# The projections of a hybrid layer rewritten: tiles in pairs by Strassen's product on half of the inner tiles, and the pairs of one head laid between the attention steps of another

## The chip, the cores and the metric

One core of one Trainium2 chip runs the kernel. The metric is the device time of one execution in microseconds (us). The time before is the median of three runs. The profiler recorded one further execution, and all rows below are of that one.

## The reference, cut to what matters

The input x is 2048 rows of 1024 numbers. One large product gives all inputs of four branches, and one gate of 1024 columns for each of them:

```python
proj = x @ w_in                       # 2048 x 1024 by 1024 x 9216
q_sb, k_sb, v_sb, g_sb, u_pool, g_pool, u_lru, g_lru, q_xa, g_xa, merge = split_columns(proj)
y_sb   = stick_breaking_attention(q_sb, k_sb, v_sb) * silu(g_sb)     # 4 heads of 128, causal
y_pool = multiscale_pool(u_pool, w_pool, pool_scale) * silu(g_pool)  # windows 2, 4, 8, 16
y_lru  = rg_lru(u_lru, ...) * silu(g_lru)                            # convolution, two gates, a scan
y_xa   = memory_cross_attention(q_xa, mem, w_mem_kv) * silu(g_xa)    # 256 memory rows
merged = sum(sigmoid(merge[n]) * (y[n] @ w_branch[n]) for n in range(4))   # 512 x 1024 each
out = layer_norm(ALPHA * x + merged @ w_out, ln_g, ln_b)
```

The attention makes for a block of 128 queries and all earlier blocks of keys the scores z, then log(1-sigmoid(z)), its sums over all later keys, and from them the weights of the values.

## The kernel before

The 2048 rows are done in two halves of 1024 (T); a half is two column blocks of 512 (C) in the moving operand. Everything is held turned, features on the partitions. A float32 product is made as three products of a finer and a coarser part: the high part is the number rounded to fp32r (ScalarE, a copy), the low part the rest (a subtraction, on VectorE or GpSimd). So XH and XL hold the half of x in 8 inner tiles, WH and WL hold one weight tile of 1024x128, and `product` runs 8 inner tiles times 3 passes times 2 blocks of 512 = 48 matmuls into two PSUM banks for one tile of 128 output columns. There are 72 such tiles in a half, taken in an order written out by hand: 16 for the heads of the attention (q, k, g, v of each), 8 gates, 8 for the pools, 8 gates, 8 for the recurrence (LRU), 8 gates, 8 for the memory attention, 8 gates. After each group of gates comes `merge`: a product of the gates' tile, then `branch`, 24 matmuls of the branch's output with w_branch, and GT and MERGED collect gate times branch on VectorE and GpSimd. The half ends with `merged @ w_out`: 8 row blocks times 2 column parts, 24 matmuls each (L662).

ScalarE splits each weight tile one tile ahead (L679), GpSimd makes its rest (L1457), SP loads the tile after that into RAW. The consumers read the PSUM banks directly, each with the operation that it needs anyway (sigmoid, scaling, high part).

The attention of a head is 12 steps in the first half and 28 in the second. A step on TensorE is three matmuls of scores (L446), two of sums (L459, L461), two of the carry to the next block (L470, L472) and one float32 product with the values (L489, two records). Step s makes the scores of block s, the sums of s-3, the values of s-4. Between them lie four activations on ScalarE, four or five operations on VectorE, one or two on GpSimd. The first steps are laid between the head's last product tile; the rest runs with no products beside it. The first products of the next head start when the last values are done.

The output weights are split while the last gates' product runs: `split_out` for the first four tiles stands in ScalarE's `merge` ahead of the last gate's sigmoid, into memory (WO0H, WO0L) that no running product reads.

TensorE takes its instructions in order, and so does each other engine. Semaphores carry every dependence.

Of the kernel before, what the change touches and what calls it, by code (L numbers as in the profile page):

```python
# [11 lines left out]
P = 128  # L12
# [5 lines left out]
C = 512  # L18
# [12 lines left out]
XP = 8  # L31
# [5 lines left out]

SET_EXP_TANH, SET_SIGMOID, SET_SQRT, SET_EXP_LN = 0, 2, 3, 6

# [3 lines left out]
PER_HALF = 4 * HEADS + 3 * 2 * HEADS + NB * FT + FT  # L43
# [7 lines left out]

POOL_OUT = [(g + 1) % 2 for g in range(4)]

SUMS, USE, EARLY = 3, 4, 4


def wait_if(engine, semaphore, count):

    if not (isinstance(count, int) and count <= 0):
        engine.wait_ge(semaphore, count)


def each(engine, first_too, n, body):


    if first_too:
        body(0)
    with engine.Fori(1 if first_too else 0, n) as i:  # L70
        body(i)


def steps_of(half):


# [8 lines left out]

def build(nc, xt, xrow, memt, w8, w4, wgate, wpool, prm, cst, ln_g, ln_b, out):
    with ExitStack() as ctx:
        base = (nc.sbuf_base + 31) // 32 * 32

        def at(name, offset, shape, dt=F32):  # L90
            return nc.alloc_sbuf_tensor_at(name, [P] + shape, dt, offset=base + offset)
# [4 lines left out]
        KIB = 1024  # L96

        XH = at("XH", 0, [KD, T], F32R)
        XL = at("XL", 32 * KIB, [KD, T], F32R)
        YH = at("YH", 64 * KIB, [KB, T], F32R)  # L100
        YL = at("YL", 80 * KIB, [KB, T], F32R)
        RAW = [at(f"RAW{i}", (96 + 4 * i) * KIB, [KD, P]) for i in range(2)]
        WH = [at(f"WH{i}", (104 + 4 * i) * KIB, [KD, P], F32R) for i in range(2)]
        WL = [at(f"WL{i}", (112 + 4 * i) * KIB, [KD, P], F32R) for i in range(2)]
        BRAW = [at(f"BRAW{i}", (120 + 2 * i) * KIB, [KB, P]) for i in range(2)]
        BH = [at(f"BH{i}", (124 + 2 * i) * KIB, [KB, P], F32R) for i in range(2)]
        BL = [at(f"BL{i}", (128 + 2 * i) * KIB, [KB, P], F32R) for i in range(2)]
        R1, R2, RC = 132 * KIB, 164 * KIB, 204 * KIB + 64
        IDENT = at("IDENT", RC, [P])
        SUFFIX = at("SUFFIX", RC + 512, [P], F32R)  # L110
        CARRY = at("CARRY", RC + 1024, [P], F32R)
        DIAG = at("DIAG", RC + 1536, [P])
        COUNT = at("COUNT", RC + 2048, [len(WINDOWS), HALO])
        PRM = at("PRM", RC + 2304, [KB, P_ALL])
        GP = at("GP", RC + 2464, [P_ALL])
        HSTATE = at("HSTATE", RC + 2528, [KB])
        LHALO = at("LHALO", RC + 2560, [KB, 4])
        PHALO = at("PHALO", RC + 2624, [KB, HALO])
        SM = at("SM", RC + 2880, [32])
        SM2 = at("SM2", RC + 3008, [64])  # L120
        STATS = at("STATS", RC + 3264, [TB, 12])


        MERGED = at("MERGED", R1, [FT, T])

        E = [at(f"E{i}", R1 + 2 * i * KIB if i < 2 else 126 * KIB, [C]) for i in range(3)]
        PF = [at(f"PF{i}", R1 + (4 + 2 * i) * KIB, [C]) for i in range(2)]
        PHI = [at(f"PHI{i}", R1 + (8 + 2 * i) * KIB if i < 3 else R2 + 36 * KIB, [C], F32R) for i in range(4)]
        PLO = [at(f"PLO{i}", R1 + (14 + 2 * i) * KIB if i < 3 else R2 + 38 * KIB, [C], F32R) for i in range(4)]
        ARG = [at(f"ARG{i}", R1 + (20 + 2 * i) * KIB, [C]) for i in range(4)]  # L130
        W = [at(f"W{i}", R1 + (28 + 2 * i) * KIB, [C]) for i in range(2)]
        VT = at("VT", R1 + 28 * KIB, [T])
        CRAW = at("CRAW", R1 + 28 * KIB, [C_ALL])
        MRAW = at("MRAW", R1 + 4 * KIB, [KD, MEM])
        MTH = at("MTH", R1 + 12 * KIB, [KD, MEM], F32R)
        MTL = at("MTL", R1 + 20 * KIB, [KD, MEM], F32R)
# [1542 lines left out]
```

## Time and profile before

| | |
|---|---|
| median of 3 runs | 2672.77 us (2671.5 to 2676.21) |
| the profiled execution's own time | 2669.68 us |
| its span | 2667.9 us |
| TensorE matmul | 2596.8 us busy, 97% |
| TensorE weight load | 2080.3 us, 78% |
| VectorE, ScalarE, GpSimd | 1072.6, 902.7, 1025.7 us |
| matmuls in the profile | 11360 |
| mean granted clock | 0.995 |

A matmul's recorded duration is longer than its place in the stream, since the next one starts while it drains. What one costs is the distance between two starts. A gap shorter than the draining doesn't show as idle time, so the span is compared with the count of matmuls too.

### The profile page before, as it was taken

The numbers are of one execution on the slowest core, as the hardware profiler recorded it, in microseconds if no ns is written. First come the engines' busy times: TensorE is split into PE (matmuls) and PEld (weight loads), VectorE is DVE, ScalarE is ACT, GpSimd is POOL, SyncE is SP. The second block draws the span as 40 slices with busy tenths as digits, with TensorE's granted clock in tenths as the row PEclk, the third lists the DMA queues.
The fourth block names the chain that finished last, engine by engine and source line by source line (L and its number), as shares of the span: only waits on it lengthen the run. The fifth ranks groups of instructions, "written<-read, shape, count | busy, mean of one in ns | idle before, by whom it ended". The sixth has DMA issues, their size and how long they took to land.

```text
span 2667.9 us, 31598 instructions
## 1 busy us (share of the span) xinstructions
PE 2596.8 (97%) x11360; PEld 2080.3 (78%) x11360; DVE 1072.6 (40%) x1701; ACT 902.7 (34%) x1496; POOL 1025.7 (38%) x654
## 2 busy tenths in 40 slices
PE   8999999999999999999999999999999999999998
PEld 7777788778877878887767767688878877888887
DVE  5545400520372034046576484701420471143056
ACT  4444411111252133122576584711121351132132
POOL 3443443433234313326344353633443234322425
PEclk9999999999999999999999999999999999999999
DMA  5111111111112111133201101011111112111131
GB/s 218 48 56 47 66 53 36 54 50 40 44 44 63 35 44 58 52 134 117 89 32 31 39 16 55 16 47 36 56 56 39 36 44 63 38 55 50 47 134 64
DMA packets 51629, 153.40 MB, mean 58 GB/s; under 512 B 5856, under 2 KB 11488, under 8 KB 51552
## 3 DMA queue, kind: packets, MB, share of 16 engines
q1 hardware_dynamic: 41472, 133.50, 15.2%
q10 hardware_dynamic: 10080, 18.88, 2.0%
q8 instruction: 48, 0.79, 0.1%
q14 instruction: 29, 0.24, 0.0%
HBM read 136.10 MB, written 16.25 MB: 57 GB/s over the span
## 4 chain that ended last, share of the span: by engine, by line
PE 81%; DVE 11%; ACT 2%; issue 2%; POOL 2%; ACTq 0%; POOLq 0%; DVEq 0%
PE PJ L399 50%; PE Z L526 7%; PE OB L526 3%; PE ACC L526 3%; PE PJ L662 2%; PE OB L489 2%; DVE XC L1317 2%; PE PJ L446 2%; PE PJ L489 1%; PE Z L446 1%; DVE PS L1275 1%; PE Z L662 1%; DVE RES L1441 1%; PE PJ L459 1%; DVE LT L1331 1%
## 5 line engine op out<-in xcount | busy, mean ns | idle before, releaser
L399 PE MATMUL PJ<-XH,WH 128*128 128x512 f32 x2304 | 715.1, 392 | 4.2 <-DVE XL L1060 4.2
L399 PE MATMUL PJ<-XL,WH 128*128 128x512 f32 x2304 | 710.8, 390 | 0.0
L399 PE MATMUL PJ<-XH,WL 128*128 128x512 f32 x2304 | 710.4, 390 | 0.0
L1457 POOL TENSOR_TENSOR WL<-RAW,WH 128x1024 fp32r<-128x1024 f32 x136 | 329.3, 2422 | 881.4 <-ACT WH L679 881.4
L399 PEld LDWEIGHTS PJ<-XH,WH 128*128 128x128 f32 x2304 | 431.1, 188 | 97.0 <-issue 8.4
L399 PEld LDWEIGHTS PJ<-XL,WH 128*128 128x128 f32 x2304 | 433.3, 188 | 90.6
L399 PEld LDWEIGHTS PJ<-XH,WL 128*128 128x128 f32 x2304 | 432.9, 188 | 90.4
L766 ACT ACTIVATE GT<-PJ 128x512 f32<-128x512 f32 x128 | 69.5, 595 | 564.0 <-PE PJ L399 564.0
L1112 DVE TENSOR_TENSOR GT<-Z,GT 128x512 f32<-128x512 f32 x64 | 41.3, 687 | 523.3 <-PE Z L526 523.3
L1533 POOL TENSOR_TENSOR PLO<-PF,PHI 128x512 fp32r<-128x512 f32 (+3 forms) x160 | 179.1, 1119 | 112.3 <-DVE PHI L1183 112.3
L679 ACT CAST WH<-RAW 128x1024 fp32r<-128x1024 f32 x134 | 140.5, 1049 | 130.7 <-PE PJ L399 130.5
L1508 POOL TENSOR_TENSOR MERGED<-MERGED,GT 128x1024 f32 (+1 forms) x62 | 150.0, 2420 | 55.6 <-DVE GT L1112 55.6
L1112 DVE TENSOR_TENSOR GT<-ACC,GT 128x512 f32<-128x512 f32 x32 | 22.1, 692 | 366.3 <-PE OB L526 366.3
L1461 POOL TENSOR_TENSOR BL<-BRAW,BH 128x512 fp32r<-128x512 f32 x64 | 82.2, 1290 | 135.3 <-ACT BH L691 135.3
L691 ACT CAST BH<-BRAW 128x512 fp32r<-128x512 f32 x64 | 39.0, 622 | 245.4 <-PE Z L526 167.2
L1477 POOL TENSOR_TENSOR ML<-MERGED,MH 128x1024 fp32r<-128x1024 f32 x28 | 68.1, 2432 | 95.4 <-ACT MH L1002 95.4
L815 ACT ACTIVATE W<-ARG 128x512 f32<-128x512 f32 (+3 forms) x160 | 89.1, 561 | 36.0 <-DVE ARG L1163 26.9
L489 PE MATMUL OB<-W,V 128*128 128x512 f32 (+2 forms) x192 | 89.0, 545 | 4.9 <-ACT W L815 4.7
L804 ACT ACTIVATE E<-E 128x512 f32<-128x512 f32 (+3 forms) x160 | 90.7, 567 | 5.4 <-issue 1.6
L670 ACT ACT_TABLE_LOAD x67 | 86.0, 1283 | 12.6 <-PE OB L608 11.5
L798 ACT ACTIVATE E<-E 128x512 f32<-128x512 f32 (+3 forms) x160 | 89.3, 558 | 0.3
L526 PE MATMUL Z<-YH,BH 128*128 128x512 f32 x256 | 80.4, 396 | 5.7 <-POOL BL L1461 5.7
(338 smaller groups left out, 3948.8 us busy)
## 6 DMA issues: line engine op xcount, KB each, us to landing
RAW<-w SPq DMA_DIRECT2D x156, 512.0 KB, 3.5
BRAW<-w SPq DMA_DIRECT2D x64, 256.0 KB, 3.2
XRAW<-xt SPq DMA_DIRECT2D x16, 512.0 KB, 10.6
RES<-xrow SPq DMA_DIRECT2D x16, 512.0 KB, 7.8
out<-RES SPq DMA_DIRECT2D x16, 512.0 KB, 2.6
MW<-w SPq DMA_DIRECT2D x8, 512.0 KB, 8.5
k_keep<-KH ACTq DMA_DIRECT2D x4, 512.0 KB, 2.7
k_keep<-KL ACTq DMA_DIRECT2D x4, 512.0 KB, 3.5
```

The source lines that it names most:

```text
L399: mm = nc.tensor.matmul(PJ[p][c][:], w[p][:, k, :], x[:, k, c * C:(c + 1) * C], start=(k == 0 and n == 0), stop=(k == KD - 1 and n == 2))
L489: nc.tensor.matmul(OUT[c][:, a:C], V[:, b, :], W[r % 2][:, a:C], start=first, stop=end, skip_group_check=True).then_inc(pv_done, 1)
L526: mm = nc.tensor.matmul(BR[p][c][:], w[p][:, k, :], y[:, k, c * C:(c + 1) * C], start=(k == 0 and m == 0), stop=(k == KB - 1 and m == 2))
L670: act.add_instruction(mybir.InstLoadActFuncSet(name=nc.get_next_instruction_name(), engine=mybir.EngineType.Activation, act_func_set_id=nu ...
L679: nc.scalar.copy(WH[p][:], RAW[p][:]).then_inc(w_hi, 1)
L798: nc.scalar.activation(e, e, ACT.Exp, scale=-1.0).then_inc(exp_done, 1)
L804: nc.scalar.activation(e, e, ACT.Ln, bias=1.0).then_inc(ln_done, 1)
L815: nc.scalar.activation(W[r % 2][:, a:C], ARG[r % 4][:, a:C], ACT.Exp).then_inc(w_done, 1)
L1457: G_.tensor_tensor(WL[p][:], RAW[p][:], WH[p][:].bitcast(F32), ALU.subtract).then_inc(w_lo, 1)
L1461: G_.tensor_tensor(BL[p][:], BRAW[p][:], BH[p][:].bitcast(F32), ALU.subtract).then_inc(b_lo, 1)
L1508: G_.tensor_tensor(d, d, GT[p][:], ALU.add).then_inc(merged, 1)
L1533: G_.tensor_tensor(PLO[s % 4][:, a:C], PF[s % 2][:, a:C], PHI[s % 4][:, a:C].bitcast(F32), ALU.subtract).then_inc(p_lo, 1)
```

## The change

**Pairs.** Two weight tiles are done together as a pair; there are 36 in a half. The inner dimension is cut: the first four inner tiles (x: B11, B12 over B21, B22; weights: the same four blocks of two tiles) go by Winograd's form of Strassen's product, seven block products of 6 matmuls; the other four inner tiles go plainly, 48 matmuls. A pair is 15 pieces of 6 matmuls, 90 in all, where two tiles took 96. Four sums of x are made once a half (T1 to T4, GpSimd), four sums of weights for every pair (`sums_raw`, GpSimd). The sums of the results are made outside TensorE: a bank that has been used in one result is copied to memory by ScalarE (`shared`, four times a pair), is accumulated further, and VectorE adds another bank to the copy (`summed`, four times a pair). The results of a pair so lie in memory, and what was made of the banks directly (sigmoid, high part) is now an operation of its own from memory.

```diff
+            def piece(g, i):                      # TensorE
+                a, c, d = (J[(g + j) % 3] for j in range(3))
...
+                if i == 0:
+                    pe.wait_ge(w_lo, 4 * g + 1)
+                    wait_if(pe, ad_done, 4 * (g - 1) + 2)
...
+                    block_product(a, ONE, 0, B11, True).then_inc(pr_done, 1)
...
+                elif i == 9:
+                    pe.wait_ge(cp_done, 4 * g + 3)
+                    block_product(a, SUMMED, 4, T3, False).then_inc(pr_done, 1)
...
+            def piece(g, i):                      # ScalarE
+                if i == 0:
+                    second_tile(g)
+                    room(g, 0)
+                    shared(g, 0, 0, 0, 1)
...
+                elif i == 9:
+                    shared(g, 1, 0, 0, 6)
+                    if not last:
+                        sums_of(g + 1)
...
+            def piece(g, i):                      # VectorE
+                if i in (4, 8, 12, 14):
+                    summed(g, (4, 8, 12, 14).index(i))
...
+            def piece(g, i):                      # GpSimd
+                if i == 0:
+                    second_tile(g)
+                elif i == 4 and not last:
+                    first_tile(g + 1, False)
+                    sums_raw(g + 1)
+                elif i == 8 and not last:
+                    first_tile(g + 1, True)
+                elif i == 9:
+                    sums_of(g + 1)
```

**Attention.** q, k and v of a head are written to device memory and are loaded again (`load_kq`, `load_v`, on ScalarE's queue) when its attention starts; splitting them is done then (`split_kq`, `rest_kq`). The attention of head h runs while the two pairs of head h+1 are made: four pieces before the first step, the others spread evenly over the steps. The last head has only the first pair of the gates. The scores have three banks in place of four.

```diff
+                for g, i in fill[:filled(half, h, -1)]:
+                    piece(g, i)
+                for s in range(ns + USE):
+                    if 0 <= s - SUMS < ns:
+                        sums(half, h, s - SUMS)
+                    if s < ns:
+                        scores(half, h, s)
+                    for g, i in fill[filled(half, h, s - 1):filled(half, h, s)]:
+                        piece(g, i)
+                    if s >= USE:
+                        values(half, h, s - USE)
+                    if 0 <= s - SUMS < ns:
+                        carry(half, h, s - SUMS)
```

**The other stages.** The work of the head before is called at set pieces of the running pair. In the memory attention:

```diff
+                # TensorE
+                    pair(g0 + XA0 + h, {9: lambda: memory_turned(half, h - 1),
+                                        12: lambda: memory_values(half, h - 1)} if h else {})
+                    memory_scores(half, h)
+                # ScalarE
+                    hooks = {9: lambda: memory_queries(half, h), 12: lambda: load_memory_values(half, h)}
+                # VectorE
+                    return {3: lambda: memory_max(half, h), 7: lambda: memory_norm(half, h),
+                            10: lambda: (silu(half, 3, h, AG[h % 2][:]), memory_turned(half, h)),
+                            13: lambda: memory_output(half, h)}
...
+                    hooks[8] = lambda: memory_queries(half, h)
```

On TensorE the hook stands ahead of its piece, on the others behind it. `memory_turned` on TensorE turns the weights into PSUM, on VectorE it copies them out (four copies of 512); `memory_values` waits for the last of these. `memory_queries` on VectorE waits for ScalarE's `memory_queries`, which stands behind `shared` and `sums_of` of piece 9.

**Output weights.** They now lie where x and its sums lie (0 to 64 KiB), so ScalarE's `split_out` waits until all products of the half are done; tiles 4 to 7 are loaded when tiles 0 to 3 have been split, since there are four raw buffers:

```diff
+                    act.wait_ge(pr_done, 8 * PAIRS * (half + 1))
+                    nc.scalar.copy(WO[k // 4][0][:, :, (k % 4) * P:(k % 4 + 1) * P], OR[k % 4][:]).then_inc(wo_hi, 1)
...
+                for k in range(FT):               # ScalarE
+                    split_out(k)
                 table(SET_SQRT)
+                split_rows(0, slice(0, 6))
...
+                    else:                         # SP, k >= 4
+                        sp.wait_ge(wo_odd if k % 2 else wo_even, half * 4 + (k - 4) // 2 + 1)
...
+                for f in (6, 7):                  # GpSimd, end of merge
+                    rest_b(half, n, f)
+                    if n:
+                        add(half, n, f - 2)
+                if n:
+                    add(half, n, 6)
+                    add(half, n, 7)
...
+                for k in range(1, FT, 2):
+                    rest_out(half, k)
```

VectorE makes the rests of the even tiles and then those of the rows. `merged @ w_out` now goes row block by row block, both column parts of one behind each other. The x of the second half is split by ScalarE in 11 units of 1024 columns (8 before), as before only after the last row product of the first half. The branches' outputs are split in four operations of 1024 columns once a branch, low parts on VectorE. Loops over heads and gates are unrolled.

## Rows read from the trace of the kernel before

**Rows 1.** The page: the span, and TensorE's busy time, share and instructions.
```profile
span 2667.9 us, 31598 instructions
PE 2596.8 (97%) x11360; PEld 2080.3 (78%) x11360; DVE 1072.6 (40%) x1701; ACT 902.7 (34%) x1496; POOL 1025.7 (38%) x654
```

**Rows 2.** Timeline of PE, product tiles: start, duration, instruction, records merged (x2).
```profile
1399.79 0.61 PE L399 MATMUL PJ<-XH,WH 128*128 128x512 f32 x2
...
1411.58 0.62 PE L399 MATMUL PJ<-XH,WL 128*128 128x512 f32 x2
```

**Rows 3.** Timeline of PE where the output product starts, first half.
```profile
1179.60 0.39 PE L526 MATMUL OB<-YH,BL 128*128 128x512 f32 x1
1179.83 0.39 PE L662 MATMUL PJ<-WO0H,MH 128*128 128x512 f32 x1
1180.06 0.39 PE L662 MATMUL PJ<-WO0L,MH 128*128 128x512 f32 x1
```

**Rows 4.** Timeline of PE: first product of a head, two heads of each half.
```profile
107.62 0.71 PE L399 MATMUL PJ<-XH,WH 128*128 128x512 f32 x1
180.51 0.47 PE L399 MATMUL PJ<-XH,WH 128*128 128x512 f32 x1
...
1387.46 0.70 PE L399 MATMUL PJ<-XH,WH 128*128 128x512 f32 x2
1498.71 0.47 PE L399 MATMUL PJ<-XH,WH 128*128 128x512 f32 x1
```

**Rows 5.** Timeline of PE: the value products of two attention steps in the second half.
```profile
1442.05 1.02 PE L489 MATMUL PJ<-W,V 128*128 128x512 f32 x2
...
1444.54 1.02 PE L489 MATMUL PJ<-W,V 128*128 128x512 f32 x2
```

**Rows 6.** Timeline of PE: float32 value products of the memory attention, four records each.
```profile
967.11 1.88 PE L608 MATMUL ACC<-PT,VM 128*128 128x512 f32 x4
968.82 1.88 PE L608 MATMUL OB<-PT,VM 128*128 128x512 f32 x4
```

**Rows 7.** Waits of PE: for whom, us in total, times, longest.
```profile
PE Z L576 <- POOL PLL L1573: 9.2, 5, 3.1
PE Z L595 <- DVE XCL L1327: 7.5, 8, 2.2
```

**Rows 8.** Timeline of PE from the last row product to the second half's products.
```profile
1269.80 0.39 PE L662 MATMUL OB<-WO1H,ML 128*128 128x512 f32 x1
...
1272.92 0.70 PE L399 MATMUL PJ<-XH,WH 128*128 128x512 f32 x2 [2.74 <-DVE XL L1060]
```

**Rows 9.** A window behind that gap: busy us of each engine, granted clock, DMA.
```profile
1274.00:1278.00 4.00, 4.00 (x12) 3.14 (x11) 4.00 (x4) 3.95 (x5) 0.00 (x0) 0.57 0.02 4
```

**Rows 10.** The page's groups: busy us, mean ns of one, idle before.
```profile
L1457 POOL TENSOR_TENSOR WL<-RAW,WH 128x1024 fp32r<-128x1024 f32 x136 | 329.3, 2422 | 881.4 <-ACT WH L679 881.4
...
L766 ACT ACTIVATE GT<-PJ 128x512 f32<-128x512 f32 x128 | 69.5, 595 | 564.0 <-PE PJ L399 564.0
...
L679 ACT CAST WH<-RAW 128x1024 fp32r<-128x1024 f32 x134 | 140.5, 1049 | 130.7 <-PE PJ L399 130.5
...
L670 ACT ACT_TABLE_LOAD x67 | 86.0, 1283 | 12.6 <-PE OB L608 11.5
```

**Rows 11.** Groups of VectorE with their shapes apart.
```profile
L1060 DVE TENSOR_TENSOR XL<-XRAW,XH 128x1024 fp32r<-128x1024 f32 x16 | 23.1, 1502 | 1.6 <-POOL RES L1612 1.4 <-ACT XH L718 0.2
...
L1399 DVE COPY PT<-Z 128x512 f32<-128x512 f32 x16 | 10.2, 681 | 0.0
...
L1347 DVE SCALAR_TENSOR_TENSOR LR<-LR,LT 128x1024 f32<-128x1024 f32 x8 | 9.8, 1226 | 0.3
```

**Rows 12.** Groups of GpSimd with their shapes apart: a subtraction of 256 columns.
```profile
L1547 POOL TENSOR_TENSOR WL<-RAW,WH 128x256 fp32r<-128x256 f32 x32 | 23.8, 742 | 0.0
```

**Rows 13.** DMA issues: KB of one, median us from issue to landing.
```profile
RAW<-w SPq DMA_DIRECT2D x156, 512.0 KB, 3.5
...
V<-v_keep ACTq DMA_DIRECT2D x4, 512.0 KB, 5.6
```

More of the change, by code:

```diff
@@ L404, in _, with pair @@
+            def pair(g, inside={}):
+                for i in range(PIECES):
+                    if i in inside:
+                        inside[i]()
+                    piece(g, i)
             for h in range(HEADS):
@@ L450, in sums @@
[L450 to L459 removed]
+                    pe.wait_ge(kq_lo, kq_count(half, h))
@@ new lines, in memory_values @@
+            def memory_values(half, h):
+                hh = half * HEADS + h
+                pe.wait_ge(pt_done, 4 * (hh + 1))
+                pe.wait_ge(vm_back, 16 * (hh + 1))
+                for c in range(NC):
+                    for m in range(MEM // P):
+                        mm = nc.tensor.matmul(BR[1][c][:], VM[:, m, :], PT[c][:, m, :], start=m == 0,
+                                              stop=m == MEM // P - 1)
+                    mm.then_inc(xo_done, 1)
+            for half in range(HALVES):
+                g0 = half * PAIRS
+                pair(g0)
+                pair(g0 + 1)
+                for h in range(HEADS):
@@ new lines, in attention @@
+            def attention(half, h):
+                ns, fill = NS[half], filling(half, h)
+                rest_kq(half, h)
+                if h:
+                    output(half, h - 1, 1)
+                silu(half, 0, h, ST[(half * HEADS + h) % 3][:])
+                for g, i in fill[:filled(half, h, -1)]:
+                    piece(g, i)
+                for s in range(ns + USE):
+                    if 0 <= s - SUMS < ns:
+                        argument(half, h, s - SUMS)
+                    if s == ENDS[half][0] + USE + 1:
+                        output(half, h, 0)
+                    if 1 <= s <= ns:
+                        softplus(half, h, s - 1)
+                    if s:
+                        for g, i in fill[filled(half, h, s - 2):filled(half, h, s - 1)]:
+                            piece(g, i)
@@ new lines, in pair, with x_sums @@
+            def pair(g, after={}):
+                for i in range(PIECES):
+                    piece(g, i)
+                    if i in after:
+                        after[i]()
+            def x_sums(half, j):
+                b11, b12, b21, b22 = XRAW[:, 0:2, 0:C], XRAW[:, 0:2, C:T], XRAW[:, 2:4, 0:C], XRAW[:, 2:4, C:T]
+                t = [x[:] for x in TR[half]]
+                for k in (0, 1) if j == 0 else (2, 3):
+                    pool.wait_ge(x_in[k], 16 * (half + 1))
+                if j in (1, 3):
+                    pool.wait_ge(t_raw, 4 * half + (1 if j == 1 else 2))
+                a, b = ((b12, b11), (b22, t[0]), (b22, b12), (b21, t[1]))[j]
+                G_.tensor_tensor(t[j], a, b, ALU.subtract).then_inc(t_raw, 1)
@@ L1550, in attention @@
[L1550 to L1565 removed]
+                ns, fill = NS[half], filling(half, h)
```

2434 lines of the change are left out of this document (1309 added, 1125 removed).

## The prediction

> **What bounds the kernel now.** The first look is the page's busy shares [rows 1]: TensorE is busy 97% of the span and nothing else is above 40%. So time can only be won by giving TensorE less to do or by closing its gaps. The second look is its timeline, for what one matmul costs. From 1399.79 to 1411.58 us there are 26 groups of two [rows 2], that is 52 matmuls in 11.79 us, 0.2267 us each; a tile of 48 takes 10.88. Where the output product starts, three passes into one bank follow each other at 0.23 us too, and the first stands 0.23 behind the last branch matmul [rows 3]: passes into one bank are no slower than passes into two, and that transition has no gap.
>
> The third look is at the heads. From first product to first product a head takes 72.9 us in the first half and 111.3 in the second [rows 4]. A full attention step there is 2.49 us long [rows 5]. Its slots on TensorE are seven times 0.2267 and one float32 product; two of those take 1.71 us [rows 6], one 0.855, so the sum is 2.44. VectorE and ScalarE have four operations of about 0.6 to 0.7 us a step each (such widths in [rows 10, 11]), so the step runs at the edge of three engines. By slots a first-half head is four tiles (43.5), six full steps (14.7) and six narrow ones (an estimate by their widths, with none under 1.0 us: 8.2), 66.4 us; a second-half head is 43.5, 22 full steps (53.7) and 8.2, 105.4. The differences, 6.5 and 5.9 us, are the ramp and the drain of the attention, which has nothing beside it. Over eight heads that is 50 us.
>
> The fourth look is at the waits: in the pool and LRU stages TensorE waits for chains of VectorE and GpSimd, 9.2 and 7.5 us in all [rows 7]. Last, between the halves TensorE stands still for 2.74 us while the new x is split [rows 8], and behind it four microseconds have a granted clock of 0.57 [rows 9], which is nearly all at 1.2 GHz. Half of that time is lost, about 1.6 us: I add it to every gap longer than some 2.5 us.
>
> **The sum, term by term, against the span of 2667.9.**
>
> *A, fewer matmuls.* 36 pairs a half lose 6 matmuls each: 72 x 6 x 0.2267 = -97.9 us. Nothing else on TensorE gets shorter; the turning of v, branches, attention and output have as many matmuls as before.
>
> *Can the others feed it?* A pair is now 20.4 us of TensorE, 1.36 a piece. ScalarE has for it two casts of 512 columns, one of 1024 (1.05) and one of 768 (0.8), and four copies of 0.6 [rows 10]: 5.5 us. VectorE has four additions out of PSUM at about 0.69 each, near the 0.68 of such a copy [rows 11]: 2.8. GpSimd has 1.3 + 1.3 + 2.4 + 1.8 us of rests, by columns from 2.42 [rows 10], and four sums of 0.74 [rows 12]: 9.8. The tightest wait inside a pair is that for WLS: piece 9 done, copy 0.6, cast 1.05, rest 2.42, with hand-overs 4.3 us, against six pieces (8.2) until TensorE wants it. A weight tile lands 3.5 us after its issue [rows 13]; it has at least half a pair. So the plain pairs cost nothing beyond their slots, and additions and copies are hidden by matmuls. If that cover were gone, each pair would lose the difference.
>
> *B, the attention.* Steps now hold 1.7 pieces on average in the first half (about 4.7 us a step) and 0.84 in the second (3.6), so VectorE's and ScalarE's 2.5 us are covered and the drain lies under the next head's pieces. What is new is the reload. ScalarE issues it when the last scores are made; two or three tiles of 512 KB land in some 6 to 7 us (from 3.5 for one [rows 13]), the high parts take 1.05 each, and the last low part 1.2 more. That is 11 to 13 us, against 13.5 (second half) to 17 of TensorE's remaining values, sums and four lead pieces. It fits, but ScalarE then still has a sigmoid, two table loads (1.28 each [rows 10]), one split and two copies ahead of the first magnitude: some 2 us late for each of three heads in the second half. With the first head of a half (the copy of the turned v stands before the next pair, 1.3) and the last heads (only 15 pieces, 2 to 3) I count 13.5 us left of the 50, after which the first product of a merge follows. Term: -36.
>
> *C, the memory attention, a new wait.* Take piece 9 of a pair done. ScalarE copies the bank (0.6), casts the summed weights (1.05) and scales q (1.05); only then can VectorE make q's low part (1.23 [rows 11]). VectorE's queue holds that ahead of the silu (1.23) and of the four copies of turned weights (4 x 0.68 = 2.7) for which `memory_values` waits. With 0.3 for hand-overs the last copy is done 8.2 us behind piece 9. TensorE has pieces 10 and 11, 2.7 us, and waits 5.5, behind which come 1.6 for the clock. What is queued behind it is everything: pieces 12 to 14 and the next scores. This holds for three pairs a half (in the fourth no q stands between): 6 x 7.1 = +42.6. The waits of this stage before (some 3 us a half, q's low part and a little) go: -6. Term: +37.
>
> *D, the output weights, a new wait.* After the last pair TensorE has four branches, 21.7 us. Count from that pair's end. GpSimd's queue puts the last addition to MERGED, which waits for the last branch, ahead of its first rest: 23.3 to 25.8. Two rests are done at 28.3 and 30.7; only then is tile 7 loaded into tile 3's buffer: landed 34.5, cast by ScalarE 35.6. Then ScalarE's table load 36.9, the cast of six eighths of a row block 37.8, VectorE's rest of that 38.8, hand-overs 0.5. TensorE stands still from 21.7 to 39.3, 17.6 us, and 1.6 for the clock. Before, the same place had no gap [rows 3]. Term: 2 x 19.2 = +38.
>
> *E, between the halves.* Before 2.74 and 1.6 us [rows 8, 9]. Now pieces 3 and 4 want five and seven units, which come at VectorE's 1.2 us each while a piece takes 1.36: 2.5 at the start, 2 in between, 2 more for the last unit, which stands behind the last row's normalisation. Term: +2.5.
>
> *F, pools, LRU, merges.* The chains of [rows 7] are as long as before, but begin a few pieces earlier. By my count VectorE's windows make the third and fourth pool pairs late by 1 to 2.5 us; each LRU pair is late by about 1.5 (convolution, silu and variance stand ahead of its last addition) and the second gates' pair behind the LRU by 2.4, since its copy goes where the scan's data lie. Some 30 us where the stages had about 36 above their slots. Term: -6.
>
> Sum: 2667.9 - 97.9 - 36 + 37 + 38 + 2.5 - 6 = 2605.6. The profiled execution lay 1.8 above its span, and the median 3.1 above that: 2610.5, I say 2611 us, 2.3% faster.
>
> **Unknown costs.** A casting copy out of PSUM into memory and an addition with a PSUM operand have near rows, so little is open. Contention is: the same kind of VectorE operation on 1024 columns takes 1.23 us alone and 1.50 while x is split [rows 11]. GpSimd goes from 1026 us [rows 1] to an estimated 1280. From below nothing is added; from above every long operation of C, D, E and F is a quarter longer, which makes C and D 5 us longer together for each half and F 20 in all: +30. I take a small part, none in the sum. The Trainium skill says in "GPSIMD Engine Reference" (key points) that GpSimd shares its SBUF interfaces with VectorE and that VectorE's instructions with two SBUF inputs contend with it. The 1.50 agrees with that; by the page nearly all low parts would be in that class, which speaks for the upper end.
>
> The skill's "TensorE: Matmul & The Clock Gate" (part 1) says that an engine that has idled runs at 1.2 GHz and returns to 2.4 only after it has been busy. The 0.57 agrees; by the page, too, the long gaps of C and D cost more than their length.
>
> **The rivals.**
> *1, C and D are hidden.* If the queues run further ahead than I read, the order costs nothing: 2611 - 75 = 2536. Against it: both chains are fixed by waits in the code and by rows. Only parts of them can be wrong; 2535 to 2580. Chance 0.14.
> *2, more waits of the kind of F.* Every pair of the pool, LRU and memory stages (24, and the four behind them) loses a further 1.5 to 2.5 us, since VectorE and GpSimd lengthen each other: 2611 + 28 x 2 = 2667, within 2640 to 2672. For it: [rows 7], where these stages already wait, and [rows 11]. Chance 0.19.
> *3, slower: attention steps bound by their chain.* With pieces in the queues of all four engines, TensorE's carry waits for VectorE's argument and its values for ScalarE's weights. If ScalarE, which waits in each step for the scores before it comes to its pieces, can't keep pace, each of 160 steps grows. It decides from 62 / 160 = 0.39 us a step; at 0.6 the time is 2707. Against it: ScalarE has some 2.9 us to do in a 3.6 us step and sums come three steps late. Chance 0.08.
> The forecast itself has 0.59; its own range is 2580 to 2640. I put the 8 in 10 range at 2560 to 2655: it leaves out the lower part of rival 1, the upper half of rival 2 and rival 3.
>
> 0.2% is about what this measurement can tell, 2667.4 to 2678.1. Faster: 0.59 + 0.14 + most of rival 2 = 0.89. Same 0.03, slower 0.08.
>
> **What would show it.** Right: 10928 matmuls' worth of slots on TensorE, pairs in the merges at 20.4 us; a wait of 5 to 6 us in TensorE's memory values for VectorE's copies, six times; a gap of 17 to 19 us ahead of the first output product in both halves, ended by VectorE's rest of the rows; heads of some 63 and 103 us. Wrong: pairs longer than 20.4 us with VectorE or GpSimd as releaser (rival 2), or steps with waits for arguments or weights in the attention (rival 3); no gaps at C and D (rival 1).

## The result and the profile after

The changed kernel takes 2689.23 us (median; 2689.08 to 2692.73, 3 runs) against 2672.77: a ratio of 1.0063, 95% interval 1.004 to 1.0086. It is slower by 0.6%, where 2611 and a range of 2560 to 2655 were forecast: the sign was wrong, by 78 us. The page of the kernel after, against [rows 1]:

```profile
span 2690.9 us, 29644 instructions
PE 2522.1 (94%) x10928; PEld 2018.4 (75%) x10928; DVE 1296.5 (48%) x1823; ACT 1139.9 (42%) x1822; POOL 1351.8 (50%) x998
```

The 432 matmuls are gone, and TensorE is busy 74.7 us less, not 97.9. So 23 us of busy time came back as slower matmuls, and the idle time rose from 71 to 169 us. Where it lies, by the waits of PE after (for whom, us in total, times, longest), against [rows 7]:

```profile
PE J L473 <- DVE ML L1627: 38.8, 2, 19.6
PE ACC L736 <- DVE PT L1608: 35.8, 6, 6.0
PE J L473 <- POOL WLS L1758: 13.8, 7, 4.2
PE ACC L612 <- POOL PLO L1820: 11.2, 8, 2.8
PE J L473 <- ACT GT L896: 10.3, 2, 5.2
...
PE J L473 <- DVE LG L1329: 7.0, 6, 1.6
PE J L473 <- ACT ST L896: 6.2, 3, 5.7
PE J L473 <- DVE XBL L1320: 6.0, 3, 2.6
PE J L473 <- DVE PG L1329: 5.7, 4, 2.3
```

The first two lines are terms D and C, each within 4 us of the waits that were forecast (35.2 and 33). The others, some 75 us with those not shown (without the start's wait for its first weights), are spread over all stages. The timeline of PE gives each stretch's length, from one merge's last branch matmul to the next one's (us, first half + second half). The output projection's stretch ends in the first half with the first product of the second half, and in the second half with the last row product. "Forecast" is the stretch before plus the terms A to F:

| stretch | before | forecast | after | after less forecast |
|---|---|---|---|---|
| first products, attention, merge 0 | 420.7 + 578.6 | 933.2 | 404.3 + 564.3 | +35.4 |
| pools, recurrence, merges 1 and 2 | 471.0 + 467.8 | 889.3 | 461.4 + 459.2 | +31.3 |
| memory attention, merge 3 | 252.4 + 252.4 | 520.0 | 267.1 + 267.2 | +14.3 |
| output projection | 93.3 + 87.3 | 218.6 | 112.2 + 109.1 | +2.7 |

With 1.2 us before the first product these are the 85 us between the sum (2605.6) and the span (2690.9). A pair in a merge is as short as reckoned: the timeline of PE after has 90 matmuls between the first product and the next branch, 20.40 us (start, duration, instruction):

```profile
367.76 0.39 PE L473 MATMUL J<-XBH,WH 128*128 128x512 f32 x1
...
388.16 0.62 PE L665 MATMUL Z<-YH,BH 128*128 128x512 f32 x2
```

Terms C and D in the same view: the memory values of the first head, behind the gap, and of the fourth head, which has none; then the place of [rows 3], the output projection's start:

```profile
950.14 3.78 PE L736 MATMUL ACC<-PT,VM 128*128 128x512 f32 x4 [5.97 <-DVE PT L1608]
953.72 2.90 PE L736 MATMUL OB<-PT,VM 128*128 128x512 f32 x4
...
1056.68 1.88 PE L736 MATMUL ACC<-PT,VM 128*128 128x512 f32 x4
1058.40 1.88 PE L736 MATMUL OB<-PT,VM 128*128 128x512 f32 x4
...
1169.55 0.39 PE L665 MATMUL OB<-YH,BL 128*128 128x512 f32 x1
1189.58 0.76 PE L473 MATMUL J<-WO0H,MH 128*128 128x512 f32 x1 [19.64 <-DVE ML L1627]
```

The predicted gaps of 5.5 and 17.6 us are 5.97 and 19.64 (19.15 in the second half). But four float32 products behind a gap take 3.58 us from start to start, where [rows 6] and the fourth head have 1.7. Windows of the kernel after (busy us of PE, PEld, DVE, ACT, POOL, then the granted clock, DMA share, GB/s) show why, behind a gap of C, one of D, and two at the start:

```profile
988.00:992.00 4.00, 4.00 (x5) 1.56 (x5) 0.00 (x0) 0.00 (x0) 0.00 (x0) 0.50 0.00 0
1189.00:1193.00 4.00, 3.42 (x8) 2.77 (x9) 1.95 (x3) 0.64 (x1) 0.00 (x0) 0.50 1.03 419
1193.00:1197.00 4.00, 4.00 (x15) 3.19 (x15) 0.00 (x0) 0.00 (x0) 0.00 (x0) 0.79 1.02 407
42.00:46.00 4.00, 3.58 (x9) 2.84 (x10) 4.00 (x2) 0.38 (x1) 4.00 (x3) 0.50 0.47 131
46.00:50.00 4.00, 4.00 (x15) 3.21 (x14) 3.99 (x4) 1.72 (x2) 2.91 (x1) 0.77 0.03 11
```

A granted clock of 0.50 is the lower level, 1.2 GHz, and 1.00 is the upper one, 2.4 GHz. At D it loses half of four microseconds and 0.21 of the next four, 2.8 us, where one window of [rows 9] had given me 1.6.

The recurrence is where the most time came back. Timelines of DVE and of POOL after, second pair of the first half:

```profile
734.06 3.37 DVE L1554 SCALAR_TENSOR_TENSOR LR<-LR,LT 128x1024 f32<-128x1024 f32 x1
...
739.82 3.30 DVE L1562 TENSOR_TENSOR LR<-LR,XC 128x1024 f32<-128x1024 f32 x1
...
743.34 3.63 DVE L1564 TENSOR_TENSOR_SCAN LT<-LA,SM,LR 128x1024 f32<-128x1024 f32 x1
...
794.37 1.23 DVE L1562 TENSOR_TENSOR LR<-LR,XC 128x1024 f32<-128x1024 f32 x1
```
```profile
733.01 3.33 POOL L1758 TENSOR_TENSOR WLS<-SR,WHS 128x1024 fp32r<-128x1024 f32 x1
736.31 1.71 POOL L1875 TENSOR_TENSOR WGL<-WGR,WGH 128x256 fp32r<-128x256 f32 x1
739.53 2.50 POOL L1879 TENSOR_TENSOR XCL<-XC,XCH 128x1024 fp32r<-128x1024 f32 x1 [1.51 <-ACT XCH L1158]
741.99 2.83 POOL L1762 TENSOR_TENSOR WL<-RAW,WH 128x768 fp32r<-128x768 f32 x1
744.78 3.27 POOL L1735 TENSOR_TENSOR WL<-RAW,WH 128x512 fp32r<-128x512 f32 x1
```

The product of L1562 takes 1.23 us while GpSimd is idle (the fourth head, 794.37) and 3.30 here. Add start and duration and follow the ends: WLS ends at 736.34, L1554 1.09 later; XCL ends at 742.03, L1562 1.09 later; WL (768) ends at 744.82, 1.70 after L1562; the scan ends at 746.97, 2.15 after that; WL (512) ends at 748.05, 1.08 after the scan. Each ends one lone duration, less 0.1 to 0.2 us, after the other engine's: whoever comes second waits for the whole instruction of the first. From one head's gate values to the next the chain over the two engines and ScalarE is 27.8 us long (721.5 to 749.2), against 23.1 us of TensorE's slots in such a pair with its gates (102 matmuls).

### The profile page after: what moved, and what is told of

It reads as the page before. It is cut to its first block, busy times and chain, and to the rows that moved or that the text cites. A ratio compares the mean times of both kernels' runs of the same rounds, so it can differ in the third digit from the quotient of the medians.

```text
span 2690.9 us, 29644 instructions
## 1 busy us (share of the span) xinstructions
PE 2522.1 (94%) x10928; PEld 2018.4 (75%) x10928; DVE 1296.5 (48%) x1823; ACT 1139.9 (42%) x1822; POOL 1351.8 (50%) x998
## 3 DMA queue, kind: packets, MB, share of 16 engines
q8 instruction: 87, 1.43, 0.2%
## 4 chain that ended last, share of the span: by engine, by line
PE 77%; DVE 10%; issue 5%; ACT 4%; POOL 3%; DMA 1%; ACTq 0%; SPq 0%; POOLq 0%; DVEq 0%
PE J L473 15%; PE J L474 15%; PE J L475 15%; PE Z L665 7%; PE OB L635 4%; PE OB L665 3%; PE ACC L665 3%; PE Z L474 1%; PE Z L475 1%; PE Z L473 1%; PE ACC L612 1%; DVE YL L1489 1%; PE ACC L614 1%; PE ACC L624 1%; PE ACC L622 1%
## 5 line engine op out<-in xcount | busy, mean ns | idle before, releaser
L473 PE MATMUL J<-XSH,WH 128*128 128x512 f32 x1152 | 454.3, 394 | 0.8 <-DVE XSL L1320 0.6
L474 PE MATMUL J<-XSL,WH 128*128 128x512 f32 x1152 | 449.1, 390 | 0.0
L475 PE MATMUL J<-XSH,WL 128*128 128x512 f32 x1152 | 449.1, 390 | 0.0
L1735 POOL TENSOR_TENSOR WL<-RAW,WH 128x512 fp32r<-128x512 f32 x144 | 222.5, 1545 | 195.3 <-ACT WH L810 180.8
L473 PE MATMUL J<-XBH,WHS 128*128 128x512 f32 x576 | 231.9, 403 | 45.5 <-POOL WLS L1758 13.8
L473 PEld LDWEIGHTS J<-XSH,WH 128*128 128x128 f32 x1152 | 217.3, 189 | 50.4 <-issue 2.1
L474 PEld LDWEIGHTS J<-XSL,WH 128*128 128x128 f32 x1152 | 217.0, 188 | 45.9 <-issue 1.9
L475 PEld LDWEIGHTS J<-XSH,WL 128*128 128x128 f32 x1152 | 216.4, 188 | 45.9
L474 PE MATMUL J<-XBL,WHS 128*128 128x512 f32 x576 | 228.5, 397 | 0.0
L475 PE MATMUL J<-XBH,WLS 128*128 128x512 f32 x576 | 228.5, 397 | 0.0
```

The costliest lines, as they stand in the source:

```text
L473: nc.tensor.matmul(to, wh, xh, start=first, stop=True, skip_group_check=True)
L474: nc.tensor.matmul(to, wh, xl, start=False, stop=True, skip_group_check=True)
L475: return nc.tensor.matmul(to, wl, xh, start=False, stop=True, skip_group_check=True)
L1735: G_.tensor_tensor(WL1[:, k, :], RAW[0][:, k, :], WH1[:, k, :].bitcast(F32), ALU.subtract).then_inc(w_lo, 1)
```

## The experiments

All are edits of the changed kernel. Times are medians, and "less" is against its 2689.2; intervals are those of the ratio to the kernel before. Lengths of stretches and waits are those of each run's profiled execution, which can lie some us from its median.

**1. The memory's queries later on VectorE.**
```diff
-                    hooks[8] = lambda: memory_queries(half, h)
+                    hooks[11] = lambda: memory_queries(half, h)
```


> One line moved on VectorE: the low half of the next head's memory queries is made after the copies of this head's turned weights, not before them. Theory 1 (the six gaps of 5.97 us at the memory values and the slow clock behind them are the whole price of term C): the gaps vanish, the memory values take 3.03 us in place of 5.9, and the span falls by 6 x (5.97 + 2.9 + 0.4) = 56 us, to about 2635 us. Theory 2 (the gaps cost only their length, the slow matmuls behind them have another reason): 6 x 5.97 = 36 us less, about 2655. Theory 3 (the wait moves to the memory scores, which now get their queries later): less than 15 us.

Measured: 2637.85 us, ratio 0.987 (0.9854 to 0.9887), 51 less. The waits at L736 are gone and the two memory stretches fall from 267.1 and 267.2 us to 240.1 each. That is 27.0 for three gaps of 5.97: 3.0 us each beyond the gap. Theory 1 holds, 5 us short of its figure. The values in the timeline of PE of this run, first head:

```profile
943.34 1.88 PE L736 MATMUL ACC<-PT,VM 128*128 128x512 f32 x4
945.05 1.88 PE L736 MATMUL OB<-PT,VM 128*128 128x512 f32 x4
```

**2. The gap left, but filled.** 26 matmuls into a free bank stand ahead of the wait; their result is not used.
```diff
+                if h < HEADS - 1:
+                    for _ in range(26):
+                        nc.tensor.matmul(JX[:], WH2[:, 0, :], XBH[:, B11, 0, :], start=True, stop=True, ...)
                 pe.wait_ge(pt_done, 4 * (hh + 1))
```


> 26 matmuls of 512 columns that nobody uses are put ahead of the memory values of heads 0 to 2, where TensorE stands still for 5.97 us; their result goes to a bank that is free there. 26 x 0.2267 = 5.9 us. Theory 1 (the slow matmuls behind a gap come from the clock that falls during it): the gap is filled, the granted clock stays up, the values take 3.03 us instead of 5.9, and the span falls by 6 x 3.3 = 20 us although the wait for VectorE is as long as before. Theory 2 (the slow matmuls come from VectorE's and GpSimd's traffic or from reading PT): nothing changes, within 3 us.

Measured: 2672.98, ratio 1.0003 (0.9994 to 1.0013), 16 less, with 156 more matmuls. Theory 1 holds: the wait for VectorE is filled and not removed, and 2.7 us a gap come back, which are the clock's alone (the memory stretches fall to 258.9 us each, 8.2 for three gaps). Timeline and windows of this run:

```profile
979.64 6.05 PE L734 MATMUL JX<-XBH,WH 128*128 128x512 f32 x26
985.78 1.99 PE L740 MATMUL ACC<-PT,VM 128*128 128x512 f32 x4
```
```profile
983.00:987.00 4.00, 3.92 (x15) 2.56 (x15) 2.73 (x5) 0.00 (x0) 0.00 (x0) 1.00 0.21 84
987.00:991.00 4.00, 4.00 (x14) 2.32 (x13) 0.10 (x1) 0.00 (x0) 0.00 (x0) 1.00 0.10 27
```

**3. The output weights early.** On each engine the splits go between the last branches; on ScalarE:
```diff
                 gate(g0 + 3, 1)
+                if n == 3:
+                    for k in range(3):
+                        split_out(half, k)
                 split_b(half, n, 6)
+                if n == 3:
+                    split_out(half, 3)
                 split_b(half, n, 7)
```
and so `rest_out` between `gated(4)` to `gated(7)` on VectorE, and ahead of `add(6)` and `add(7)` on GpSimd.

> The splits of the output weights are put between the last two branch products on all three engines, and the first row tile's splits between those of the weights. Theory 1 (term D is only a matter of order): the two gaps of 19.6 and 19.2 us ahead of the output projection fall to under 2 us each and with the clock behind them (about 3 us each) the span falls by 40 us, to about 2650. Theory 2 (the weights' transfers or the crowding of VectorE and GpSimd bound it whatever the order): half of it stays, 15 to 25 us less.

Measured: 2665.56, ratio 0.9976 (0.9966 to 0.9985), 24 less. That is theory 2's range, yet not its cause. The waits of PE keep two gaps in each half:

```profile
PE J L473 <- DVE ML L1642: 7.0, 2, 3.5
PE J L473 <- POOL WO1L L1909: 6.9, 2, 3.5
```

GpSimd's rests stood behind its additions still, and the transfers into their buffers behind them. This order was not yet the right one: in run 8 the two stretches, 221.3 us in the changed kernel, are 186.9. Since run 8 also moves three of the splits to VectorE, it does not show order alone.

**4. The sixth product back.**
```diff
-                    block_product(a, ONE, 0, B11, True).then_inc(pr_done, 1)
+                    block_product(a, ONE, 0, B11, True)
+                    block_product(a, ONE, 0, B11, True).then_inc(pr_done, 1)
```


> The first block product of every pair is issued twice, so that a pair has 96 matmuls of 512 columns again; everything else is as in the changed kernel. Theory 1 (TensorE bounds every stage, so term A is worth its slots): 72 x 6 x 0.2267 = +97.9 us, about 2788. Theory 2 (in the stages where TensorE waits for VectorE, GpSimd and ScalarE, the six matmuls fall into idle time): less, by up to the idle time of some 30 us in pairs that wait, +65 to +85 us.

Measured: 2762.83, ratio 1.0338 (1.0321 to 1.0356): 73.6 us more for 97.9 us of slots. Theory 2. The waits for WLS fall from 13.8 us to 4.4, those for LG from 7.0 to 2.8, for PG from 5.7 to 1.4. The recurrence's two stretches grow by 5.8 and 5.1 us where the slots are 10.9. (The memory stretches grow by 8.8 and 7.8: there a part falls into the gaps of C.)

**5. Small sums of weights on GpSimd.** Only 4 of 128 columns are summed, so the result is another.
```diff
+                n = P if g % PAIRS == 0 else 4
-                a11, ... = RAW[0][:, 0:2], ...
+                a11, ... = RAW[0][:, 0:2, :n], ...
```


> GpSimd's four sums of weights of each pair but the first of a half are made on 4 of 128 columns of each block (the rest of the sums is left as it is in the tile, so the products are not the reference's); all other work and every wait stay. Takes away 70 x 4 x (0.74 to 1.7) us of GpSimd's work. Theory 1 (the new sums crowd VectorE and GpSimd, and this is what makes the recurrence, the pools and the start longer than their slots): the waits for the summed weights (13.8 us) and part of those in the recurrence (some 15 us) go, and the span falls by 15 to 30 us. Theory 2 (the waits come from the order of the old work against shorter pairs): under 5 us.

Measured: 2679.11, ratio 1.0024 (1.0015 to 1.0034), 10 less: a miss for both. The attention stretches lose 14 us (399.8 and 554.7), and there the waits for PLO fall from 11.2 us to 1.9. The recurrence does not change (243.2, 242.8), nor do the waits for WLS (13.8). So the new sums are not what crowds the recurrence.

**6. Another order in the recurrence.**
```diff
-                act.wait_ge(y_f, y_count(half, 2, h))          # ahead of the gate values
+                wait_if(act, l_scan, hh)                       # l_scan: behind the scan
-  12: (silu(half, 2, h - 1, ...), variance(half, h - 1))
+  12: (variance(half, h - 1), silu(half, 2, h - 1, ...))
```
and `gate_values` goes behind ScalarE's fifth piece; the tanh waits for `y_f`.

> In the recurrence: the gate values wait for the scan and not for the two products behind it, the variance comes ahead of the silu product on VectorE, and ScalarE's copy of the shared product comes ahead of the gate values. Theory 1 (these pairs are bound by a chain over VectorE, ScalarE and GpSimd of 27.8 us a head, of which 24.1 to 26 remain): the chain loses 2.0 + 1.7 us in each of three heads and up to 5 us at the merge of each half, so the span falls by 2 x (3 x 3 + 5) = 20 to 30 us. Theory 2 (TensorE's own slots and slow clock make these stages long): under 5 us.

Measured: 2680.14, ratio 1.0026 (1.0015 to 1.0037), 9 less. The stretches lose 3.2 and 4.5 us, not ten or more: the wait at the merge falls only from 5.2 to 3.1, and the waits for WLS rise from 13.8 to 15.9, and that low half stands behind the square in GpSimd's queue (run 11 moves the square). Reordering the chain took out little.

**7. Another order at the start.**
```diff
-            for u in range(6, NU):
+            for u in range(6, 9):
                 unit_hi(0, u)
-                    pair(g0)
+                    pair(g0, {1: (unit_hi(0, 9), unit_hi(0, 10)), 5: keep_memory(0), ...})
```


> At the start ScalarE copies the first shared products before it splits the last two sums of x and before it issues the twelve transfers of the memory's keys and values, and GpSimd makes the first sums of weights ahead of the second sum of x. Theory 1 (the 15.4 us above the slots are two waits, 4.2 and 5.7 us, with the slow clock behind each): both shrink, 8 to 13 us less. Theory 2 (VectorE and GpSimd are too crowded there for any order): 0 to 3 us less.

Measured: 2683.21, ratio 1.0045 (1.003 to 1.006), 6 less. The first stretch falls from 404.3 to 395.0. It begins 1.8 us later, but so it does in runs 1, 3 and 6, which leave the start alone, so this is not the edit's. A new wait of 4.0 us for GpSimd's low half of the first tile stands there: a part of the gain only changed who is waited for.

**8. All orders together,** with three odd splits of the output weights moved to VectorE and one semaphore for each buffer.

> The orders of the earlier runs together: the queries later, the output weights early (with three of the odd splits moved from GpSimd to VectorE and the first row tile's split ahead of them on ScalarE), the recurrence's and the start's. If the gains add: 51 + 24 + up to 15 more at the output weights + 20 + 8, that is some 115 us below the changed kernel, 2570 to 2585 us, below the kernel before as well. If the waits hide one another, 2590 to 2610.

Measured: 2589.99 (2588.58 to 2593.3, 5 runs), ratio 0.9694 (0.968 to 0.9707): 3.1% faster than the kernel before, 99 us less than the changed one. The gains of 1, 3, 6 and 7 add to 90, and the output weights, with another order than in run 3 and less work on GpSimd, give the rest: those stretches are 94.8 and 92.1 us now (112.2 and 109.1). The largest waits left:

```profile
PE J L473 <- POOL WLS L1775: 13.4, 8, 1.9
PE ACC L612 <- POOL PLO L1837: 10.9, 8, 2.8
PE ACC L473 <- POOL KWL L1813: 9.5, 1, 9.5
PE J L473 <- ACT GT L896: 6.3, 2, 3.1
```

**9. A quiet GpSimd.** As run 5, and the low halves of the weights on 4 of 128 columns too.
```diff
-                G_.tensor_tensor(WLS[:], SR[:], WHS[:].bitcast(F32), ALU.subtract).then_inc(w_lo, 1)
+                n = P if g % PAIRS == 0 else 4
+                G_.tensor_tensor(WLS[:, :, :n], SR[:, :, :n], WHS[:, :, :n].bitcast(F32), ...).then_inc(w_lo, 1)
```


> As the fifth run, and GpSimd's low halves of the weights too are made on 4 of 128 columns, but for the first pair of a half; the rest of each tile is left as it was, so the products are not the reference's. Every wait and all of VectorE's work stay. The waits fall into two kinds: those on GpSimd itself (summed weights 13.8 us, low halves of p 11.2) and those on VectorE and ScalarE in pairs (16.9 us on the recurrence's and the merge's tiles, 5.7 in the pools, 6 between the halves). Theory 1 (the two engines lengthen each other): VectorE's operations of 1024 elements in the recurrence fall from 2.8 us to 1.23 and the scan from 3.3 to 2.35, both kinds of waits go, and with the clock the span falls by 45 to 65 us. Theory 2 (the order of work is the cause): only the first kind goes, 20 to 35 us.

Measured: 2618.36, ratio 0.9803 (0.9788 to 0.9818), 71 less, beyond theory 1's range. VectorE has the same instructions, but 133 us less busy time; the page of this run and one of its groups with its shape, first the same group of the kernel after:

```profile
L1564 DVE TENSOR_TENSOR_SCAN LT<-LA,SM,LR 128x1024 f32<-128x1024 f32 x8 | 26.5, 3308 | 0.3
```
```profile
PE 2498.5 (95%) x10928; PEld 2010.8 (77%) x10928; DVE 1163.4 (44%) x1823; ACT 1140.1 (44%) x1822; POOL 766.1 (29%) x998
...
L1564 DVE TENSOR_TENSOR_SCAN LT<-LA,SM,LR 128x1024 f32<-128x1024 f32 x8 | 18.8, 2351 | 0.3
```

The recurrence's stretches are 225.4 and 225.6 (17 and 18 us shorter), the pools' 212.7 and 212.3. Waits for VectorE go with those for GpSimd: LG from 7.0 to 2.1, PG from 5.7 to 0.2, YL to nothing, and ScalarE's LU to nothing as well. The waits for ML at the output projection and for ST at the start (6.6 us) remain. The run takes away two things at once, GpSimd's own time in TensorE's path and the lengthening of VectorE; run 12 parts them.

**10. All orders and the sixth product,** runs 8 and 4 together.

> All orders of the eighth run, with the first block product of every pair issued twice, as in the fourth run. Against the eighth run (2590 us): theory 1 (the 24 us by which the fourth run fell short of 97.9 lay in waits that the new matmuls filled): fewer of them are left, so the price of the 432 matmuls is closer to their slots, +80 to +95 us, 2670 to 2685. Theory 2 (a matmul issued twice on the same operands costs less than its slot): +74 again, 2664.

Measured: 2660.43, ratio 0.9961 (0.995 to 0.9971), 70 more than run 8: theory 1's figure missed, and yet theory 2 doesn't hold. The memory stretches, which have no wait left, grow from 240.0 and 240.1 to 251.0 each, 10.9 us and so exactly the 48 slots; the recurrence's stretches grow by 0.7 and 3.9 us. In all the waits for WLS fall from 13.4 to 3.0. A matmul costs its slot where TensorE is the bound, and 0.7 or 3.9 of 10.9 us in the recurrence, even with the better order.

**11. The square on ScalarE,** in run 8's kernel, and one more order at the start.
```diff
+                act.wait_ge(l_act, 2 * hh + 2)
+                nc.scalar.activation(LR[:], LA[:], ACT.Square).then_inc(l_sq, 1)
-                        hooks[7] = lambda: squared(half, h - 1)     # GpSimd
```


> All orders of the eighth run, and the square in the recurrence moves from GpSimd to ScalarE, where it stands right behind the tanh; at the start two more splits of x stand behind ScalarE's first copies and GpSimd's second sum of x behind its first low halves. Theory 1 (the chain through GpSimd's square, 1.9 us and two hand-overs a head, and what stands behind it in GpSimd's queue keep the recurrence longer than its slots): 8 to 15 us under the eighth run, 2575 to 2582 us. Theory 2 (the summed weights' waits have another cause): within 4 us of it.

Measured: 2582.77 (5 runs), ratio 0.9673 (0.9659 to 0.9686), 7 less than run 8, just under theory 1's range. The recurrence's stretches fall from 240.0 and 237.9 to 233.1 and 234.1, the waits for WLS from 13.4 to 0.7; the waits for ScalarE's copy LG rise from 3.8 to 10.4 us and take part of their place. The new order at the start gained nothing (398.6 us for 398.0). This is the fastest version.

**12. One input instead of two.** GpSimd's low halves of weights become a product of the raw tile with a constant, so they are others.
```diff
-                G_.tensor_tensor(WLS[:], SR[:], WHS[:].bitcast(F32), ALU.subtract).then_inc(w_lo, 1)
+                G_.tensor_scalar(WLS[:], SR[:], 0.001, None, ALU.mult).then_inc(w_lo, 1)
```


> In the changed kernel GpSimd's three kinds of low halves of the weights (two inputs, raw and high) become products of one input with a constant, at full width, so they are not the reference's; the four sums and all else stay. GpSimd is then still busy at the same places. Theory 1 (the lengthening comes from two engines with two inputs each in the same memory at once): VectorE's operations of the recurrence get their lone times back (scan 2.35, 1024 elements 1.23) wherever only these operations ran beside them, and the span falls by 40 to 70 us, near the ninth run. Theory 2 (any work of GpSimd lengthens VectorE's): VectorE's total stays near 1296 us in place of 1163, and the span falls only by what GpSimd's own operations become shorter, 0 to 25 us.

Measured: 2651.42, ratio 0.992 (0.9903 to 0.9936), 38 less, just short of theory 1's range. The page of this run:

```profile
PE 2507.5 (95%) x10928; PEld 2015.9 (76%) x10928; DVE 1202.2 (45%) x1823; ACT 1140.1 (43%) x1822; POOL 1406.4 (53%) x998
```

GpSimd is busy 55 us more than in the changed kernel, and VectorE 94 less, 71% of what run 9 gave it; the scan's mean is 2.54 us. The pools' and the recurrence's stretches are 30 us shorter together (890.4 for 920.6). So it is not GpSimd's being busy as such that lengthens VectorE's operations. But theory 1 doesn't hold to the end: one input on GpSimd still lengthens them, only by less. Timelines of VectorE and of GpSimd in this run:

```profile
774.18 2.05 DVE L1554 SCALAR_TENSOR_TENSOR LR<-LR,LT 128x1024 f32<-128x1024 f32 x1
774.02 2.86 POOL L1758 TENSOR_SCALAR WLS<-SR 128x1024 fp32r<-128x1024 f32 x1
```

L1554 takes 2.05 us here, where it took 3.37 beside the subtraction and takes 1.21 alone, and it ends 0.65 us before GpSimd's operation does, not 1.1 behind it. The scan takes 2.61 us beside such an operation (2.35 alone, 3.63 before). L1562 stays at 3.3 us, since it still meets the subtraction XCL, which this run left as it was; so the 71% is no exact share. The Trainium skill, "GPSIMD Engine Reference" (key points), names two SBUF inputs on VectorE's side as a condition of this contention. The runs agree: VectorE's additions with one input in PSUM stay at 0.68 us beside GpSimd. That GpSimd's second input counts too is what this run adds.

## Why the prediction was wrong, step by step

Three steps failed. F took the other engines' operations at lone durations and found most of their chains covered: 31 us of the miss. B took the attention's overlap as nearly free and left out the waits at the start and those for GpSimd's PLO: some 34. And the slow clock behind a gap was put at half its price, which made half of the 14 of C. Together they turned a gain of 62 us into a loss.

**A, slots.** 10928 matmuls and 20.40 us a pair, as forecast. That their removal is worth -97.9 is wrong: 73.6 in run 4, 70 in run 10. "So the plain pairs cost nothing beyond their slots" holds for plain pairs. What failed is that it was carried over to all pairs. Its check compared busy times of one engine at a time with a pair's 20.4 us, at lone durations. Where a pair also carries a head's recurrence or pool, the chain over the other engines sets its length, and slots taken from TensorE there come back as waits.

**F, pools, recurrence, merges,** was that mistake in figures: -6 forecast, +25 measured (920.6 us after, 938.8 before, 43.5 of slots). My 1.5 us for each recurrence pair were 1.0 in the first of them and 4.3 to 5.5 in the next three of each half (24.1, then 27.4 to 28.7 us for 23.1 of slots), and the 2.4 at the merge was a wait of 5.2. Run 9 takes 45 us out of these stretches, more than the whole miss of 31; run 5 shows that in the recurrence the low halves do it and not the sums; run 12, with GpSimd no less busy, takes out 30, so that most of it is the lengthening of VectorE's operations and not GpSimd's own time. I had this risk in view as rival 2, as the "+30" of the unknown costs and as what the Trainium skill says of contention, but sized it as "a quarter longer" from a mean of 1.50 us. That mean hid that an operation which finds GpSimd in the midst of one waits for its end: 3.30 us for 1.23. And it lengthens GpSimd as well, by 1.4 to 2.5 times.

**B, the attention:** -36 forecast, about -2 measured (without the change in slots the two stretches grew by 1.9 us, in which E alone has 3.6). Heads come at 64.0 and 64.3 us in the first half (63 forecast), but at 105.5 to 106.1 in the second (103). The start lost 15.4 us over its 162 matmuls, in waits of 4.2 us for GpSimd and 5.7 for ScalarE with the slow clock behind each; I had priced the new x only between the halves. Run 7 takes back 9 us of that stretch. GpSimd's PLO is waited for once in the first half's last head (2.8 us) and in every head of the second (1.6 to 1.9 each, and more in the last); by my count the last heads lost 4.4 and 8.5 us instead of 2 to 3. Run 5, in which these waits all but go, takes back 14. These two runs make 23 of the miss; the rest of it was not tried one by one.

**C, the memory attention:** place and cause right. The size (5.97 for 5.5) is in part luck. VectorE's low half of q, priced at its lone 1.23 us, met GpSimd's WLS and took twice that; ScalarE's operations, the copies and the hand-overs were 0.9 shorter than reckoned:

```profile
944.02 2.54 DVE L1599 SCALAR_TENSOR_TENSOR XQL<-XQR,XQH 128x1024 fp32r<-128x1024 f32 x1 [4.96 <-ACT XQH L1199]
```

In runs 9 and 12, where it takes 1.23 us, the gaps are 4.7. The clock was mis-sized: 3.0 us behind each gap by run 1, 2.7 by run 2, where I had 1.6. The whole measured term is 2 x (267.1 - 252.4) + 21.8 = +51, for +37; of the 14 between, the clock is 7 to 8 and the longer gaps 3; the rest is open.

**D, the output weights:** place and cause right, 19.6 and 19.2 for 17.6; GpSimd's first rests, reckoned at 2.4 us each, took 3.3 beside VectorE's. With the clock (2.8) the stretches grew by 40.7 us in all for 38.4.

**E, between the halves:** the same place, but longer. A wait of 2.47 us at the start, then 7.07 us above the slots over the first 162 matmuls, with further waits of 0.6, 0.9 and 2.6 and the slow clock in it: 9.5 for 6.5 reckoned. Before it was 6.2 and not 4.3, since a second wait of 1.43 us was overlooked, so the term is +3.4. (Its own figures, 6.5 against 4.3, make 2.2 and not the 2.5 that was put down.)

**Rival 2** named what happened; its 56 us for those stages are too many (31), and none of it fell on the memory stage's pairs: in run 1 their stretches, 240.1 us, are even shorter than before less the slots (241.5). But the same cause also worked in the attention, and the clock came on top. **Rival 1** would have held only with the queues reordered: run 8 is that kernel, and its 2590 us are not 2536, since the pairs' waits stay. **Rival 3** did not occur: TensorE waited 0.2 us for arguments in the whole run, and not for weights.

## What to carry to other kernels

Before counting removed matmuls as gain, ask for each stage whether TensorE is its bound: issuing the removed work again, on the side, prices it (here 10.9 us of 10.9 in one stage, 0.7 and 3.9 in another). When an engine's load on a shared memory grows, take the durations of the other from rows that stand beside such an operation, not from means. And give each gap on TensorE its length and the slow clock behind it; moving one line in a queue was worth more here than half of the Strassen saving.

## What the runs showed of the hardware

- VectorE and GpSimd, with two inputs each in SBUF, take turns by whole instructions: VectorE's 1024 columns take 1.23 us or up to 3.37 in the timeline above, the scan 2.35 or 3.63, GpSimd's 1024 columns 2.40 or 3.33, its 512 columns 1.29 or 3.27. VectorE's additions with one input in PSUM stay at 0.68 us. The Trainium skill says in "Trainium Architecture — The Big Picture" (what this means for kernel authors) that this shared port pair is an exclusive lock and not a split of bandwidth; the ends worked out above agree with it.
- With one input on GpSimd (run 12) VectorE's operation is held up for less than GpSimd's whole instruction: 2.05 us for 1.21, ending 0.65 us before it; the scan's mean is 2.54 us. GpSimd's own operation is not shorter for it (2.87 us for 1024 columns on the mean, 2.65 with two inputs).
- Gaps of 4 to 20 us on TensorE are followed by a granted clock of 0.50 for the first four microseconds and of 0.77 and 0.79 in the next four, in the windows above; 2.7 to 3 us are lost behind one. A shorter wait can have it too: behind the one of 1.84 us for WLS at 736.4 the window 737.40:740.60 has 0.50. Filled with unused matmuls (run 2), a gap costs its length alone.
